# Two layers of differential attention: the order of maximum and join, of scores and transpositions, and of three copies

## The reference, cut to what matters

```python
def diff_attention(q, k, v, lam):
    ...
        sc = jnp.einsum("bqmhd,bkmhd->bmhqk", qi, k,
                        preferred_element_type=jnp.float32) * scale
        q_idx = i * Q_BLOCK + jnp.arange(Q_BLOCK)
        mask = key_idx[None, :] <= q_idx[:, None]
        p = jax.nn.softmax(jnp.where(mask, sc, -jnp.inf), axis=-1)
        a = p[:, 0] - lam * p[:, 1]
        return jnp.einsum("bhqk,bkhe->bqhe", a.astype(v.dtype), v)
    ...

    q = apply_rope(q.reshape(b, s, 2, N_DIFF_HEADS, DIFF_HEAD_DIM), cos, sin)
    k = apply_rope(k.reshape(b, s, 2, N_DIFF_HEADS, DIFF_HEAD_DIM), cos, sin)
    ...
    o = rmsnorm(o, diff_subln_g) * (1.0 - lam_init)
```

## Time and profile before

| | |
|---|---|
| median of 3 runs | 1890.86 us (1890.68 to 1891.1) |
| profiled execution | 1890.01 us, its span 1888.2 us |
| PE busy | 1858.5 us, 98% of the span |
| DVE, ACT, POOL busy | 45%, 39%, 59% |
| the chain that ended last | PE 89%, DVE 7%, ACT 2% |
| granted TensorE clock, mean | 0.997 |

### The profile page before, as it was taken

The page is one execution under the profiler, slowest core; times in us unless marked ns, Lnnn a source line. Parts: engine busy times, 40 slices in busy tenths (PEclk is TensorE's granted clock), DMA queues, the critical chain, the costliest instruction groups (busy, mean ns, idle before and its releaser), DMA issues.

```text
span 1888.2 us, 28786 instructions
## 1 busy us (share of the span) xinstructions
PE 1858.5 (98%) x8588; PEld 1498.0 (79%) x8588; DVE 848.0 (45%) x1374; ACT 728.5 (39%) x1159; POOL 1106.1 (59%) x1310
## 2 busy tenths in 40 slices
PE   8999999999999999999999999999999999999998
PEld 6776678888888888767888888888867888888886
DVE  7777643455555121876533333112776533333112
ACT  5245553432332222476433232223476432322222
POOL 5442235667667665776556556666776555655663
PEclk9999999999999999999999999999999999999998
DMA  7211112222222333322222222332322222222322
GB/s 253 76 58 46 57 55 97 96 89 100 100 92 97 103 108 100 112 62 73 90 95 95 100 97 91 103 109 101 115 70 62 90 99 94 97 99 93 104 104 78
DMA packets 52405, 177.47 MB, mean 94 GB/s; under 512 B 6832, under 2 KB 8112, under 8 KB 52080
## 3 DMA queue, kind: packets, MB, share of 16 engines
q1 hardware_dynamic: 52336, 176.57, 28.1%
HBM read 168.84 MB, written 2.10 MB: 91 GB/s over the span
## 4 chain that ended last, share of the span: by engine, by line
PE 89%; DVE 7%; ACT 2%; DVEq 1%; issue 1%; DMA 0%; SPq 0%; ACTq 0%
PE bank L571 23%; PE bank L551 23%; PE bank L552 23%; PE bank L608 3%; PE bank L609 3%; PE bank L615 3%; DVE bank L1447 2%; PE bank L799 1%; PE bank L846 1%; PE bank L832 1%; PE bank L591 1%; PE bank L585 1%; PE bank L586 1%; PE bank L660 1%; PE bank L970 1%
## 5 line engine op out<-in xcount | busy, mean ns | idle before, releaser
L496 POOL TENSOR_TENSOR wl<-raw,wh (+1 forms) x1244 | 1018.3, 849 | 755.5 <-ACT wh L1044 755.2
L1044 ACT ACTIVATE wh<-raw 128x1024 fp32r (+1 forms) x311 | 329.8, 1060 | 815.2 <-PE bank L571 683.1
L551 PE MATMUL bank<-xh,wh 128*128 128x512 f32 x1336 | 524.4, 393 | 2.4 <-ACT lv L1044 2.4
L552 PE MATMUL bank<-xl,wh 128*128 128x512 f32 x1336 | 521.3, 390 | 0.0
L571 PE MATMUL bank<-xh,wl 128*128 128x512 f32 x1336 | 338.7, 393 | 0.0
L551 PEld LDWEIGHTS bank<-xh,wh 128*128 128x128 f32 x1336 | 251.3, 188 | 60.2 <-issue 4.5
L571 PEld LDWEIGHTS bank<-xh,wl 128*128 128x128 f32 x1336 | 248.4, 188 | 58.6 <-issue 8.5
L552 PEld LDWEIGHTS bank<-xl,wh 128*128 128x128 f32 x1336 | 251.4, 188 | 51.6
L551 PE MATMUL bank<-hh,wh 128*128 128x512 f32 x528 | 205.4, 389 | 0.0
L552 PE MATMUL bank<-hl,wh 128*128 128x512 f32 x528 | 205.4, 389 | 0.0
L1495 DVE TENSOR_TENSOR ybuf<-bank,rstd 128x512 f32<-128x512 f32 x95 | 65.3, 688 | 239.6 <-PE bank L571 237.6
(11 more groups left out here) (300 smaller groups left out, 2174.8 us busy)
## 6 DMA issues: line engine op xcount, KB each, us to landing
raw<-in_weights SPq DMA_DIRECT2D x311, 512.0 KB, 3.4
turned<-ybuf SPq DMA_DIRECT2D x64, 64.0 KB, 2.0
xs<-in_x SPq DMA_DIRECT2D x4, 512.0 KB, 6.7
out_t<-xs SPq DMA_DIRECT2D x8, 256.0 KB, 2.0
w1k<-in_w SPq DMA_DIRECT2D x1, 1024.0 KB, 9.7
w1v<-in_w SPq DMA_DIRECT2D x1, 1024.0 KB, 11.2
shifted<-kvraw SPq DMA_DIRECT2D x8, 124.0 KB, 2.3
posi<-in_positions SPq DMA_DIRECT2D x2, 256.0 KB, 8.9
```

Of the source, the lines that this page charges most:

```text
L496: x_ = pool.tensor_tensor(wl[:, :, :].rearrange("p s n -> p (s n)")[:, two], raw[:, cols((v % 4) * (CB * P) + h * part, part)], wh[:, :, : ...
L551: mm(b[:, :], w, kh(k), start=first and k == 0, stop=False)
L552: mm(b[:, :], w, kl(k), start=False, stop=False)
L1044: return act.activation(o, i, ACT.Copy, scale=scale)
```

## The change

Three pieces of code trade places:

- VectorE, `map_step`: in a slot, `peak` of block i now stands ahead of `combine` of block i - 1.
- TensorE, `head_step`: `score_l` of block i now stands ahead of `turn_l` of block i - 2.
- ScalarE, slot 22: the copies of two value banks now stand ahead of `chunk_end` (the high part of tile 12) and of `products`.

```diff
@@ TensorE
                 def head_step(h, step):
 
+                    if step < 4:
+                        score_l(h, step)
                     if 2 <= step < 6:
                         turn_l(h, step - 2)
-                    if step < 4:
-                        score_l(h, step)
@@ ScalarE
                         for h, step in steps:
                             head_step(h, step)
+                        if s == 22:
+                            for i in range(2):
+                                act.wait_ge(R["v_psum"], Count(i + 1).loop(l, 2).value())
+                                copy(lv[:, :, i, :], VB[i][:, :].rearrange("p (h d) -> p h d", d=P),
+                                     scale=s_recip[:, i:i + 1]).then_inc(R["v_out"], 1)
                         if half == 0 and n > 4:
                             chunk_end(n - 1)
@@ VectorE
                 def map_step(h, step):
+                    if step < 4:
+                        peak(h, step)
                     if 1 <= step < 5:
                         combine(h, step - 1)
-                    if step < 4:
-                        peak(h, step)
```

More of the change, by code:

```diff
@@ L1412, in _ @@
                             y_head("ya0", ya[:, 0, :])
[L1413 to L1417, removed]
                         if s == 38:
```

## The result

The changed kernel takes 1906.47 us (median of 4 runs, 1902.9 to 1906.55) against 1890.77 of the kernel before beside it: a ratio of 1.0079, with a 95% interval of 1.0067 to 1.0091. It is slower, as forecast, but by 15.7 us where 5.2 were forecast, and it lies above the range of 1892.2 to 1900.8. The profiled execution took 1906.44; that of before took 1890.01. So 16.4 us are to be found.

A forecast was written before the change was run, and what follows sets the result against it. TensorE, busy 98% of the span, was taken as the bound. Per layer -0.6, +0.2, +0.6, 0, +1.4 and +1.0 gave 2.6, for two layers 5.2: 1895.2 profiled, 1896.1 on the median's scale; range for all 1892.2 to 1900.8.

The forecast's parts named there:

- five places: TensorE's waits at tile 12 and in slots 26, 30, 34 and 38, where the prediction worked out the change's effect.
- Tile 12: Behind ScalarE's moved value copies: wait of 1.19 becomes about 0.6, ended by `wh`, giving back 0.6 a layer.
- Scores ahead of the turn: TensorE's swapped order, 16 pairs: 0.8 in all on either side, taken as 0; earlier scores counted elsewhere.
- I take one for the two layers as before: Clock behind slot 38: one half-clock stretch costing 1.7 in the two layers, unchanged from before.
- second rival: More half clock: waits in slots 34 and 38 bring two further stretches of 1.7, giving 1899.5; chance 0.17.
- Slot 26: Join of block 2 ends at 813.5, TensorE's turn waits about 0.6; TensorE then 0.2 behind the old time.
- 0.3 longer: Slot 26's bound: if this join and the one before are each 0.3 longer, TensorE is 0.8 behind.
- Slot 30: Score of head 2: `lk` 0.6 or 0.7 later, replacing exponentials as the last; TensorE stays 0.15 behind.
- Slot 34: Largest term: join delays `lk` to 6.75 behind the scores' start; net 1.4 a layer, bounds 0.9 to 2.0.
- Slot 38: Join behind slot 36's maximum delays the reciprocals, and TensorE's spread, by 0.97 a layer; bounds 0.5 to 1.4.
- first rival: Moved joins stay hidden in VectorE's slack, only the copies count: 1890 to 1893.3; chance 0.20.
- I cost it at nothing: Same shift in slots 27, 28, 31, 32 and 35: work behind it has a slot or more to spare.

The follow-up runs named there:

- join first in four slots: Changed kernel with the join ahead of the maximum again in slots 25, 29, 33 and 36 only; 1890.87 us, ratio 1.0.
- all but the maximum: Changed kernel with VectorE's `map_step` as before, so only the copies and scores moved; 1887.24 us, ratio 0.9985.

## Why the prediction was wrong

**Right.** The direction; the five places and what ends each wait; that VectorE's swap is behind the whole loss and the two other edits give a little. Tile 12 waits 0.65, ended by `wh`, for 0.6 forecast. In slot 24 the score starts 0.3 later by the trace, which began 0.84 later; on the old scale that is 804.55, as forecast. Scores ahead of the turn cost nothing measurable (ratio 0.9993, with 1 in its interval).

**The step that failed first: "I take one for the two layers as before".** There were four half-clock stretches, and two of them were twice as long as the one I had measured: 10.2 us for 1.7. This is 8.5 of the 11.2 us by which the profiled execution missed its 1895.2. The second rival had the mechanism, at a chance of 0.17, and too small a price: it took two more stretches of 1.7, 1899.5. The argument against it, that the wait of 1.44 had brought none, rested on one place in one trace. The same place had a stretch behind waits of 1.52 (join first in four slots) and 1.91 (all but the maximum), first layer both times. The kernel with unused products settles it: when TensorE is kept at work through these waits, 9.6 us come back by the medians.

**The second: the lengths in slots 26 and 30.** TensorE's waits rose by 4.25 a layer for the 2.6 forecast, 3.3 us in all. The bounds that I gave for single slots add up to 4.2 a layer (I wrote 4.0), so that the waits alone came out at the upper end.
- Slot 26: 0.6 forecast, 1.32 found. The joins of slots 24 and 25 took 1.77 and 1.68 with their small instructions, for 1.2 and 1.46. So the first was 0.57 longer, more than the "0.3 longer" of my bound, and the turn came 0.97 behind its old time for a bound of 0.8.
- Slot 30: forecast no net change; the wait went from 1.44 to 2.27. The shift by the join was sized rightly, but the rotation's first pass, 0.80 before in slot 29, took 1.67 because it now began within an addition of GpSimd. I had moved it and kept its length.
- Slot 34: 1.4 forecast, 1.39 found; `lk` was ready 6.73 behind the start of the scores for 6.75 in the working. This is partly luck. The first pass grew by 1.0 and the last shrank by 0.9 (1.61 to 0.69), since they had changed places beside the additions.
- Slot 38: from 0.52 to 1.77, so 1.25 for 0.97 forecast, within its bounds. From the maximum of slot 36 (872.10 after, 866.82) to the reciprocals (882.00, before 875.45) it is 9.90 for 8.63.

The trace of before already held the warning. A join's pass over 256 columns took 0.48 in slot 35, and in slot 28 this:

```profile
824.78 1.53 DVE L1447 SCALAR_TENSOR_TENSOR lp<-lp,small 128x256 f32<-128x256 f32 x1
```

My bounds for slot 34 went by 0.48 and 0.88, the shortest and the longest pass in the rows that I had picked.

The changed kernel without additions shows the cause of the first three: their passes shrink to 0.49 (slot 24) and 0.62 to 0.69, and the waits for `lk` and the joined map vanish. So the first rival, hidden joins, had nearly the outcome that comes without GpSimd's additions (0.6 us between the two kernels by the medians); it was these that decided against it.

**"I cost it at nothing" (the other slots)** was wrong by some 3.6 us at most, measured from the other side, with the four decisive joins back in place; 1.3 of it is seen in the traces.

## What to carry to other kernels

A duration read from a trace belongs to the place where it was read. For a VectorE pass with two operands in SBUF, look up what GpSimd does at its new time, and carry both lengths, the free one and the one behind a GpSimd instruction, into the sum. Where TensorE bounds the kernel and a change adds pauses of 1 to 2 us between narrow products, price each pause twice, once as the wait and once as a stretch at half clock behind it, and compare the loss with a version that keeps TensorE at work in the pause. A forecast that finds each new wait in its place can still be short by a factor of three.

## What the runs showed of the hardware

- A pass of VectorE is held to the end of a GpSimd addition that was issued first: rotation 1.67 for 0.66, `lk` 1.58 to 1.61 for 0.69, a join of 384 columns 1.10 and 1.11 for 0.62. The other way round, an addition took 1.72 for 1.29. Beside GpSimd's subtractions for `wl` such a join took 1.02 (slot 29 after) and 1.19 (slot 33 before), and the 1.19 stays when the additions are left out.
- The length of a wait alone does not tell whether the clock falls. After, the wait of 2.27 at slot 30 was followed by a stretch at 1.2 GHz in the first layer and by none in the second, that of 1.39 at slot 34 by none in the first and by one in the second. The windows behind the two that stayed at 2.4 GHz, slot 34 of the first layer and slot 30 of the second:

```profile
861.00:867.00 6.00, 5.86 (x33) 4.46 (x34) 3.60 (x11) 4.39 (x13) 4.92 (x6) 1.00 0.01 4
1416.00:1424.00 8.00, 6.60 (x36) 5.08 (x37) 5.78 (x12) 6.21 (x17) 4.25 (x6) 1.00 0.11 28
```

The Trainium skill, "TensorE: Matmul & The Clock Gate", section "HAM oscillation — how this bites in real kernels", has the clock halved when TensorE waits for data between bursts, and the next burst started slow; the waits of its example are longer than those here. The changed kernel shows the same in slot 38 of both layers (0.66), where four narrow products of the spread follow a wait of 1.77; the two windows above, behind waits of 1.39 and 2.27, do not.
